# Sixteen more weight quarters of the modulation as row products on VectorE

## The reference

```python
sc, scc = jax.nn.silu(c), jax.nn.silu(c_ctx)
for l in range(2):
    shift, scale, gate = jnp.split(sc @ w_ada[l] + b_ada[l], 3, axis=-1)
    shift_c, scale_c, gate_c = jnp.split(scc @ w_ada[l] + b_ada[l], 3, axis=-1)
    h = rms(x, norm_w[l]) * (1.0 + scale[:, None]) + shift[:, None]
    hc = rms(xc, norm_w[l]) * (1.0 + scale_c) + shift_c
    ...
    x = x + gate[:, None] * merge_out(o_a, o_b, o_c, z, w_out[l])
```

## Time and profile before

| | |
|---|---|
| median of 3 runs | 3220.66 us (3220.47 to 3222.27) |
| profiled execution | 3219.77 us, span 3218.0 us, mean granted clock of PE 0.999 |
| PE busy | 3178.2 us (99%) |
| DVE busy | 2344.6 us (73%) |
| ACT busy | 1452.3 us (45%) |
| POOL busy | 718.6 us (22%) |
| L2334, modulation on PE | x448 records, first at 872.5 us, last at 1548.9 us |
| L1955, row products on DVE | x64, first at 1626.3 us, last at 2231.7 us |

### The profile page before, as it was taken

One profiled execution on the slowest core, in us unless ns is written; L12 is line 12 of the kernel. 1 busy time (PEld: TensorE's weight loads), 2 busy tenths in 40 slices (PEclk: granted clock), 3 DMA queues, 4 the chain that ended last, 5 costly groups with the idle time before them and its releaser, 6 DMA issues.

```text
span 3218.0 us, 54543 instructions
## 1 busy us (share of the span) xinstructions
PE 3178.2 (99%) x19414; PEld 2719.3 (85%) x19414; DVE 2344.6 (73%) x3407; ACT 1452.3 (45%) x2240; POOL 718.6 (22%) x632
## 2 busy tenths in 40 slices
PE   8999999999999999999999999999999999999999
PEld 8988988888998888889888787788778888888878
DVE  7888877667877777777776776567668776876765
ACT  5444446554444343444542433533452363543453
POOL 5999940111450000000300011001211100210200
PEclk9999999999999999999999999999999999999999
DMA  6555555565577777676633332134236543424434
GB/s 230 183 183 183 184 188 188 190 213 183 197 247 249 269 245 271 233 266 233 228 134 112 112 120 96 53 125 147 94 105 209 201 160 116 133 92 144 161 111 166
DMA packets 159868, 559.63 MB, mean 174 GB/s; under 512 B 17552, under 2 KB 23840, under 8 KB 159264
## 3 DMA queue, kind: packets, MB, share of 16 engines
q1 hardware_dynamic: 154144, 534.60, 48.6%
q0 software_dynamic: 5504, 22.04, 2.1%
HBM read 550.26 MB, written 6.31 MB: 173 GB/s over the span
## 4 chain that ended last, share of the span: by engine, by line
PE 64%; issue 20%; DVE 7%; DVEq 3%; ACT 2%; POOL 1%; POOLq 1%; DMA 0%; ACTq 0%; SPq 0%
PE psum L2278 13%; PE psum L2282 13%; PE psum L2279 13%; PE psum L2305 10%; PE psum L2306 5%; DVE wlo L1426 3%; PE psum L2655 3%; PE psum L2681 2%; PE psum L2665 2%; DVEq L1412 1%; POOL thirdcat L2845 1%; PE psum L2461 1%; POOLq L2898 1%; ACT whi L905 1%; DVEq L1638 1%
## 5 line engine op out<-in xcount | busy, mean ns | idle before, releaser
L1426 DVE TENSOR_TENSOR wlo<-raw,whi 128x1024 fp32r<-128x1024 f32 (+3 forms) x844 | 1047.4, 1250 | 313.3 <-ACT whi L905 284.6
L905 ACT ACTIVATE whi<-raw 128x1024 fp32r<-128x1024 f32 (+3 forms) x844 | 862.3, 1028 | 891.9 <-DMA raw<-in_stream 382.2
L2278 PE MATMUL psum<-hcat,whi 128*128 128x256 f32 (+1 forms) x2924 | 975.2, 334 | 3.6 <-DVE wlo L1426 2.8
L2282 PE MATMUL psum<-hcat,wlo 128*128 128x256 f32 (+1 forms) x2924 | 964.5, 330 | 0.8 <-DVE gate_half L1955 0.8
L2279 PE MATMUL psum<-hcat,whi 128*128 128x256 f32 (+1 forms) x2924 | 964.5, 330 | 0.0
L2305 PE MATMUL psum<-hcat,whi 128*128 128x512 f32 x2560 | 904.6, 398 | 2.3 <-POOL hcat L2845 0.9
L2306 PE MATMUL psum<-hcat,wlo 128*128 128x256 f32 x2560 | 717.8, 280 | 0.0
L2278 PEld LDWEIGHTS psum<-hcat,whi 128*128 128x128 f32 x2924 | 555.2, 190 | 64.1 <-issue 11.0
L2282 PEld LDWEIGHTS psum<-hcat,wlo 128*128 128x128 f32 x2924 | 555.1, 190 | 52.4 <-issue 1.2
L2279 PEld LDWEIGHTS psum<-hcat,whi 128*128 128x128 f32 x2924 | 555.4, 190 | 49.5 <-issue 0.5
L2305 PEld LDWEIGHTS psum<-hcat,whi 128*128 128x128 f32 x2560 | 480.5, 188 | 126.2 <-issue 9.3
(11 more groups left out here) (326 smaller groups left out, 3469.4 us busy)
## 6 DMA issues: line engine op xcount, KB each, us to landing
raw<-in_stream SPq DMA_DIRECT2D x978, 512.0 KB, 3.5
raw<-in_stream SPq DMA_DIRECT2D x18, 384.0 KB, 3.0
raw<-in_stream SPq DMA_DIRECT2D x24, 256.0 KB, 3.0
resid_dram<-X POOLq DMA_DIRECT2D x2, 2048.0 KB, 9.6
crow<-c_dram POOLq DMA_DIRECT2D x4, 1024.0 KB, 9.3
bias<-in_natten POOLq DMA_DIRECT2D x16, 256.0 KB, 2.9
X<-resid_dram POOLq DMA_DIRECT2D x4, 1024.0 KB, 6.0
raw<-in_stream SPq DMA_DIRECT2D x16, 192.0 KB, 2.6
```

What stands on the lines that cost most here:

```text
L905: act.activation(whi[:, c % HI_SLOTS, 0:n], raw[:, slot, 0:n], ACT.Copy).then_inc(hi_ready, 1)
L1426: vec.tensor_tensor(wlo[:, slot, 0:n], raw[:, slot, 0:n], whi[:, c % HI_SLOTS, 0:n].bitcast(F32), ALU.subtract).then_inc(lo_ready, 1)
L2278: pe.matmul(dst, h, cat[:, kk, c0:c0 + width], start=(q == 0 and k == 0), stop=False)
L2282: last = pe.matmul(dst, l_, cat[:, kk, c0:c0 + width], start=False, stop=(q == nq - 1 and k == nch - 1))
```

## The change

The modulation keeps its 160 quarters and its arithmetic. Two blocks (18 and 19, the second half of layer 1's scale) move from PE to row products. The groups 0 and 3 of the feed-forward part lose the two clusters of four quarters among their down tiles, and two of the 14 blocks go. b0 gets one row quarter after each of its tiles 2 to 9, zb0 one after each of its tiles 0 to 5, c0 two after its tile 2. `ROW_CHUNKS` goes from 16 to 24. Before, the first halves were the quarters of a0, za0 and b0 (6 + 6 + 4) and the second halves those of c0 (16). Now the first halves are a0, za0 and b0 (6 + 6 + 12), the second halves zb0 and c0 (6 + 18).

```diff
 MOD_FEW = [0, 0, 0, 4] * 4 + [0] * LATE + [0, 4, 0, 0, 0, 4, 0, 0, 0, 0, 0, 0, 0]
 MOD_FEWER = [0, 0, 0, 4] * 4 + [0] * KD
-MOD_GROUPS = [MOD_FEW] * 4 + [MOD_FEWER]
+MOD_GROUPS = [MOD_FEWER, MOD_FEW, MOD_FEW, MOD_FEWER, MOD_FEWER]
...
-ROW_MODS = dict(a0=[2, 2, 0, 0, 0, 0, 0, 0, 0, 0, 1, 1], za0=[1] * 6, b0=[2, 2, 0, 0, 0, 0, 0, 0, 0, 0], c0=[2, 2, 0, 2, 2, 2, 1, 1, 2, 1, 1])
+ROW_MODS = dict(a0=[2, 2, 0, 0, 0, 0, 0, 0, 0, 0, 1, 1], za0=[1] * 6, b0=[2, 2, 1, 1, 1, 1, 1, 1, 1, 1], zb0=[1] * 6 + [0, 0], c0=[2, 2, 2, 2, 2, 2, 1, 1, 2, 1, 1])
```

## The result

The changed kernel takes 3233.01 us (median of 6 runs, 3232.45 to 3235.15) against 3220.56 us for the kernel before on the same chip (6 runs). The ratio is 1.0039, interval 1.0029 to 1.0050: slower by 12.5 us. The forecast was 3229.9 us. The profiled execution has a span of 3230.8 us, 12.8 more than before. I split those 12.8 us by the starts of the same instruction in both traces: where the distance between the two changes, time is lost or won. In the later experiments, one execution of a changed kernel (9122.61 us) and two of the kernel before beside it (3881.30 and 7492.75 us) took far longer than all others, and are left out of every median and ratio.

The account below looks back on a forecast made before the run. PE, busy all the time, was taken as the bound. -9.1 (work off PE) + 16.6 (wait at zb0) + 1.7 (clock) = +9.2 us on 3219.77 gave 3229.0, forecast as a median of 3229.9 us; 8-in-10 range 3218 to 3238.

Parts of the forecast that it names:

- the deciding term: Start of zb0: PE's first scores delayed by 16.6 us, through DVE's lag and the late second load of crow0.
- The wait at the start of zb0: Late load and two products hold DVE's stage, delaying PE's first scores 16.6 us, 5.7 us of b0 included.
- DVE's tile in b0: A quarter adds 2.28 us; DVE falls behind PE 1.89 us in tile 2, then 1.72 a tile, 14.0 after tile 9.
- the meeting with POOL: In b0's tiles 3 to 9 a row product meets POOL's rope instruction: 0.5 us a tile, bounds 0 and 0.77.
- PE's waits for L1976: In b0 the late sums make PE wait from its tile 6 on, about 5.7 us by the end.
- The clock: PE's idling before zb0's first scores lowers its granted clock once: +1.7 us, bounds 0 and twice that.
- I take the same price in group 3: Removing group 3's down-tile clusters saves PE 2.05 us each, as in group 0; both groups with transposes together -9.1 us.
- The further row products of zb0 cost 0: In zb0, row products beyond the first cost PE 0, as za0 has one quarter per tile with PE always busy.
- the attention of zb0 is delayed too: Rival: row products delay PE up to 2.84 us in each of zb0's tiles 1 to 5, at most +14; chance 0.07.
- The rest of layer 0: Other costs: c0's added products 0, at most one meeting of 0.8 us; the DMAs 0.

Follow-up runs that it names:

- The last experiment: Kernel with b0's quarters in a0 and group 3's up-tile clusters removed, but zb0's tiles 1 and 6 freed, c0 taking two more quarters: 3210.03 us, ratio 0.9970.
- group 4: The changed kernel, but group 3 keeps its down-tile clusters and group 4 loses two clusters among its up tiles: 3230.45 us, ratio 1.0031.
- the lag taken out: The changed kernel, but six of b0's row quarters (tiles 2 to 7) move to za0, two after each tile there: 3231.03 us, ratio 1.0031.
- the load's wait alone: The kernel before, but two of c0's second halves move to tiles 0 and 1 of zb0: 3225.65 us, ratio 1.0016.

## Why the prediction was right, and where its steps were off

The forecast of slower held, by the mechanism named as the deciding term. The steps:

- **The wait at the start of zb0, +16.6: measured 15.3.** The order was right: lag, rope, load, products, stage, scores. DVE went on 5.8 us after the load's issue instead of 6.7, which explains 0.9 of the 1.3; the issue was 14.6 us late instead of 15.0, which is the rest. The experiments split the term: 7.7 us by the lag (quarters behind the stage), and 7.6 more by the quarter in front of the stage once the lag is there (2.4 without it).
- **DVE's tile in b0.** The growth was foreseen at 1.72 us a tile and is 1.68; the meeting with POOL at 0.5 and is 0.55. The rule of the Trainium skill, page "SBUF — State Buffer", section "Who interferes with whom", as the prediction reads it, would have made it 0.74, the whole POOL instruction, since both start together (1930.56 and 1930.57): the kind of the interference agrees, its size is smaller here. The page of the Trainium skill says "for the whole instruction" of VectorE's 2-port modes, and of two SBUF inputs only that they contend. Tile 2 was taken at 1.89 us and cost 1.18: I had counted the 0.39 us before one copy as all the slack there was, but in that tile DVE also waited 0.74 us for ACT (L951) before its reciprocal. The lag ends at 12.7 instead of 14.0.
- **PE's waits for L1976, 5.7 by the end of b0.** 4.0 us in three waits, before tiles 7, 8 and 9, one tile later than said. The wait for the last copy, L2643, 2.8 us, was not in my list, but it lies in front of the same scores and is part of the 15.3. The three entries of the list that lie before the scores make 12.7 of it. Of the other 2.6 us 1.6 are the clock, which fell before the stage: from L2643 to the last L2282 in front of the scores PE takes 4.61 us, and 3.02 with the same work at a clock of 1.00 in the kernel with zb0's quarters behind the stage. The last 1.0 lies in pauses too short for the list, which I have not taken apart.
- **The clock, +1.7: measured 1.8.** The value was borrowed from one wait behind c0 and fits, which is partly luck; in the other kernels that waited there it was 1.5, 2.1 and 2.5.
- **"I take the same price in group 3": this step failed.** The two blocks were to bring 9.1 us and brought 5.4 (5.3 in the sum, since the trace was 0.14 us late before them). Group 0 brought 4.4 of 4.5; group 3 brought 1.0. Its down tiles run beside the context pairs: DVE scales (L1484), ACT normalises (L999, L1002) and only then converts two weight quarters (L905), DVE makes their low parts (L1426) and scales again. The timelines of DVE and ACT after the change:

```profile
1423.06 0.69 DVE L1484 TENSOR_TENSOR scaled<-X,rst 128x512 f32<-128x512 f32 x1
...
1426.59 1.22 DVE L1426 TENSOR_TENSOR wlo<-raw,whi 128x1024 fp32r<-128x1024 f32 x1 [1.69 <-ACT whi L905]
...
1429.20 0.68 DVE L1484 TENSOR_TENSOR scaled<-X,rst 128x512 f32<-128x512 f32 x1
```

```profile
1423.81 1.09 ACT L999 ACTIVATE hfull<-scaled,ada_t,gain 128x256 f32<-128x256 f32 x2 [2.44 <-DVEq L1486]
1424.98 0.63 ACT L1002 ACTIVATE hcat<-hfull 128x512 fp32r<-128x512 f32 x1
1425.51 1.99 ACT L905 ACTIVATE whi<-raw 128x1024 fp32r<-128x1024 f32 x2
```

  Both engines wait for each other, and a turn takes 6.13 us for two down tiles. PE needs less for them (5.8 us: the distance of 6.13 between 1427.96 and 1434.09, less the 0.31 us by which it stops), and now it stops once a turn:

```profile
1415.22 0.36 PE L2278 MATMUL psum<-thirdcat,whi 128*128 128x256 f32 x1 [0.15 <-DVE wlo L1426]
...
1421.83 0.35 PE L2278 MATMUL psum<-thirdcat,whi 128*128 128x256 f32 x1 [0.62 <-DVE wlo L1426]
...
1427.96 0.36 PE L2278 MATMUL psum<-thirdcat,whi 128*128 128x256 f32 x1
```

  The matmuls stand 0.12 us apart within a tile, and at eight places of this stretch 0.33 to 0.91; the surplus adds up to 3.0 us, which is nearly what is missing. In the kernel before the turn was already 6.13 us where no cluster stood, but the two clusters, 2.05 us each, held PE back long enough for the low parts to be ready:

```profile
1408.48 0.68 DVE L1484 TENSOR_TENSOR scaled<-X,rst 128x512 f32<-128x512 f32 x1
1415.23 0.68 DVE L1484 TENSOR_TENSOR scaled<-X,rst 128x512 f32<-128x512 f32 x1
1421.85 0.68 DVE L1484 TENSOR_TENSOR scaled<-X,rst 128x512 f32<-128x512 f32 x1
1428.38 0.68 DVE L1484 TENSOR_TENSOR scaled<-X,rst 128x512 f32<-128x512 f32 x1
1434.52 0.68 DVE L1484 TENSOR_TENSOR scaled<-X,rst 128x512 f32<-128x512 f32 x1
```

  The clusters start at 1412.98 and 1426.53: 6.75, 6.62 and 6.53 us around them, 6.14 behind. That the up tiles of the same group give 4.5 to 4.8 us confirms that it is the place and not the group. I had read PE's 761.34 of 762 us as "PE sets the pace everywhere", but a second chain of nearly the same length lay right beneath it. That the ring is the cause is shown by its pace in both traces and by the group's other half; a kernel with a shorter ring was not tried.
- **"The further row products of zb0 cost 0": they cost 1.0.** One of the six, in tile 1, stands between a normalisation and the mask of the next pair, and PE waits for ACT's exponentials. It is the rival "the attention of zb0 is delayed too", with one tile of five and a third of its price. The last experiment removed it.
- **The rest of layer 0 at 0:** right for a0, za0 and c0 as the change has them.

The miss of 3.1 us on the median has these parts: 3.8 lost in the feed-forward part (3.5 of it in group 3), 1.0 in zb0, 0.1 for the clock, against 1.3 less at the scores, on spans; the medians differ by 0.5 less. The 1.3 hid part of the error in group 3; the direction did not hang on it, for with group 3's price right the forecast would have been more strongly slower.

So the change failed by where the quarters stood: with them in a0 and behind the stage it gains 6.4 us (3220.14 to 3213.70), and with the second block out of group 3's up tiles and tile 1 free 9.9 us (3219.90 to 3210.03 on the same chip).

## What to carry to other kernels

Before work is put on an idle engine, read the idle time per step and what stands behind the added work: the 21 us that DVE was idle in b0 held only 1.06 us a tile before the copy, against the 2.28 that a quarter adds, while in a0 it was 2.40 in most tiles, and there sixteen products were free. An instruction that waits for a transfer must not stand in front of a signal that others need; moving it behind the signal gave back over 7 us without moving any work. And an engine that is busy 100% does not give back what is taken from it if a ring of two others runs only a few per cent faster: look for waits with regular spacing on the others, and compare their period with the engine's own before counting a gain.

## What the hardware did that I had not expected

- The length of a wait of PE did not decide whether the clock fell. Behind 2.3 us before its first scores it was lower (0.72 from 1984 to 1988 us and 0.85 in the 4 us behind; the scores took 2.08 us instead of 1.13), and behind 2.77 us for L2004 in the changed kernel (0.73 from 1982 to 1986), but behind the same 2.77 us, after the same waits, it stayed at 1.00 in the kernel with zb0's quarters behind the stage.
- The price grew much less than the wait before the scores: 1.5 us behind 2.3 us of waiting, 1.8 behind 5.9, 2.1 and 2.5 behind 6.2 and 6.3.
- The same load of 1024 KB landed 6.7 us after its issue in the kernel before, and 5.7, 5.7, 6.5 and 7.4 in the four kernels where DVE waited for it (the changed one, group 4, the lag taken out, the load's wait alone).
- A row product that starts together with POOL's 0.74 us instruction takes 0.55 us longer, not 0.74. In a0, with POOL idle, the same product always takes 1.28.
